# Sparse attention scores from three products of rounded query and key parts

## The chip, the cores and the metric

The kernel runs on one NeuronCore of a Trainium2 chip. The metric is the time of one execution on the device in microseconds (us). TensorE (PE in the profile) multiplies matrices into PSUM, VectorE (DVE), ScalarE (ACT) and GpSimd (POOL) work elementwise, SyncE (SP) issues transfers. Each engine runs its own queue in program order, and they meet at semaphores.

## The reference, cut to what matters

The program is a trunk of two layers on 512 tokens of width 1024: a gated DeltaNet mixer and a SwiGLU network, then a sparse attention mixer and another SwiGLU network. All of it is float32. The change lies in the attention of the second layer, whose core is:

```python
q = (c_q @ w_uq).reshape(B, S, DSA_HEADS, DSA_QK_DIM)        # 16 heads of 64
...
q_lat = jnp.einsum('bqhd,hdc->bqhc', q_b, w_uk)
s = jnp.einsum('bqhc,bqkc->bqhk', q_lat, kv_sel).astype(jnp.float32) * (DSA_QK_DIM ** -0.5)
s = jnp.where(valid[:, :, None, :], s, -jnp.inf)
p = jax.nn.softmax(s, axis=-1).astype(kv_sel.dtype)
o_lat = jnp.einsum('bqhk,bqkc->bqhc', p, kv_sel)
o = jnp.einsum('bqhc,hcv->bqhv', o_lat, w_uv)
```

Each query attends to 128 keys that an indexer has picked, from itself backwards. The kernel computes the scores against all keys up to the query's block and masks those not picked, and it multiplies the latents with `w_uk` first, so that queries and keys meet as vectors of 64 per head.

## The kernel before, in words

Queries `q_t` and keys `k_t` (L253, L255) are float32 tiles of 128 lanes x 8 head pairs x 512 tokens: lanes 0 to 63 hold one head of a pair, lanes 64 to 127 the other. There are 8 head pairs `i` and 4 query blocks `b` of 128 tokens; block `b` needs (b + 1) x 128 keys. A unit `u = 4 i + b` is one block of one pair.

For each unit TensorE computes the scores of both heads into two PSUM banks (`att_scores`, L2843). VectorE adds the mask and takes the row maximum (`masked`, L2958), ScalarE takes the exponentials (`att_exps`, L2855), TensorE transposes them (`turn`, L2868), ScalarE and VectorE copy one head each out of PSUM (`turned_out`, L2944 and L2946), and TensorE multiplies with the values (`values`, L2880). In TensorE's program step `t` is: scores of unit t, transposes of unit t-3, values of unit t-4. Once a pair there are the sums of the exponentials: VectorE's reciprocal and its rounded parts (L2972 to L2975), a transpose (L2888), ScalarE's copy, a broadcast product (L2894), VectorE's scaling (L2981), ScalarE's rounding `o_t_hi` (L2935) and VectorE's remainder `o_t_lo` (L2988). The order on every engine is written out by hand. Waits that matter here: scores of unit u wait until unit u-2 is masked (two pairs of banks), masking of unit u waits for the transposes of unit u-3, and the transposes of unit u wait until the copies of unit u-1 are out.

The first two units are computed inside `dsa_v_pe`, ahead of the last two of eight products that make the value tile `v_tok` (L2759 copies it out). At that time VectorE is at the indexer's top-k (MAX8 in L2819, MATCH_REPLACE in L2822), and the masking of unit 0 comes behind it.

All large products of the kernel use fp32r, a rounded form of float32: a number is split into a rounded part hi (written as F32R by a copy) and a remainder lo (a subtraction), and hi·hi + hi·lo + lo·hi is summed. The scores and the values of the attention are multiplied in plain float32 instead.

GpSimd makes the remainders of the first half of the output weights during the attention (`out_split`, L395, one after each of ScalarE's four `out_split_act` in steps 6, 10, 14 and 18), then rounds the second half (`out_hi_pool`, L705), whose remainders VectorE makes behind the attention. Behind it TensorE runs the output product (`pe_out`, L782 to L784). `qi_t` (L292) holds the indexer's queries in the place `h_base`, used until the last indexer logits.

Of the kernel before, what the change touches and what calls it, by code (L numbers as in the profile page):

```python
# [14 lines left out]
F32R = mybir.dt.float32r  # L15
ALU = mybir.AluOpType
# [3 lines left out]
P = 128  # L20
# [58 lines left out]
def build_trunk(nc, x, c, ada_w, ada_b, norm_g, ffn_w_in, ffn_w_out,  # L79
# [3 lines left out]
    _, S, D = x.shape  # L83
    DC = D // P
    NB = S // P
# [6 lines left out]
    AH, DH, LAT = dsa_w_uk.shape[1:]  # L92
    LC = LAT // P
    IH = dsa_w_qidx.shape[2] // DH
# [18 lines left out]
    with ExitStack() as ctx:  # L113
# [3 lines left out]
        def fixed(name, shape, dt=F32, at=None):  # L117
            size = 4
            for n in shape[1:]:
                size *= n  # L120
            size = (size + 31) // 32 * 32
            if at is None:
                at = place[0]
                place[0] += size
                assert place[0] <= nc.sbuf_usable_end, name
            t = nc.alloc_sbuf_tensor_at(name, shape, dt, offset=at)
            return t
# [48 lines left out]
        h_base = place[0]  # L176
# [75 lines left out]
        q_at = dsa.at  # L252
        q_t = dsa("q_t", [P, 8, S])  # L253
        k_at = dsa.at
        k_t = dsa("k_t", [P, 8, S])  # L255
# [34 lines left out]
        CB = [cb_gdn, cb_late, cb_late, cb_late]  # L290
        LATE = [late_gdn, late_ffn, late_dsa, late_ffn]
        qi_t = fixed("qi_t", [P, 4, S], at=h_base)  # L292
        mask = fixed("mask", [P, NB, S], at=h_base + 8192)
        v_tok = fixed("v_tok", [P, NB, 1024], at=h_base + 16384)
        relu = fixed("relu", [P, IH, S], at=ada_base)
# [3 lines left out]
        ps = ctx.enter_context(nc.psum_tensor("ps", [P, 8, S], F32))  # L299
# [3 lines left out]
        def sem(name):  # L303
            if name not in sems:
                sems[name] = ctx.enter_context(nc.semaphore(name))
            return sems[name]
# [16 lines left out]
        def f32(t):  # L323

            return t.bitcast(F32)
# [66 lines left out]
        def split(eng, ops, q, s, kc=8, src=None, dst=None):  # L392
            eng.wait_ge(hi_done, q * 4 + s + 1)
            lo, hi = (split_tile(w, s, kc) if dst is None else dst(w) for w in (w_lo, w_hi))
            ops.tensor_tensor(lo, raw_tile(s, kc) if src is None else src, f32(hi),  # L395
                              ALU.subtract).then_inc(lo_done, 1)
# [191 lines left out]
        def pool_root(pool, n):  # L588
            pool.wait_ge(sem("row_made"), 1 + 16 + n + 1)
            nc.gpsimd.tensor_tensor(rinv[:, NB * n:NB * n + NB], var[:, 0:NB], half[:, 0:NB], ALU.pow)\  # L590
                .then_inc(sem("row_root"), 1)
# [31 lines left out]
        def pool_first_root(pool):  # L623
            pool.wait_ge(sem("row_made"), 1)
            nc.gpsimd.tensor_tensor(row_rinv[:, 0, :], row_var[:, 0, :], half[:, 0:NB], ALU.pow)\
                .then_inc(sem("row_root"), 1)
# [55 lines left out]
        def out_views(m, q, s):  # L682

            if q == OUT_Q[m]:
                return raw_half(s), lambda w: w[:, s, :]
            late = LATE[m]
            if OUT_K[m] == DC:
                return raw_half(s), lambda w: late[0 if w is w_hi else 1][:, s, :]
            return flat(raw[0][:, :, :])[:, s * S:(s + 1) * S], \
                lambda w: late[0 if w is w_hi else 1][:, s // 2, (s % 2) * S:(s % 2 + 1) * S]  # L690
# [5 lines left out]
        def out_split(eng, ops, m, q, s):  # L696
            src, dst = out_views(m, q, s)
            split(eng, ops, q, s, src=src, dst=dst)
# [924 lines left out]
        def gdn_pool(pool):  # L1623

            load_ada(pool, 0, 4)
            load_ada(pool, 0, 5)
            load_ada(pool, 0, 6)
            load_ada(pool, 0, 7)
            pool_k_root(pool)
            load_ada(pool, 0, 8)  # L1630
            load_ada(pool, 0, 9)
            pool_strict(pool)
            for m in range(UNITS):
                pool_eu(pool, m)
            pool.wait_ge(sem("eu_made"), UNITS)
            nc.gpsimd.memset(xq[0:32, :, 32:64], 0.0).then_inc(sem("x_zero"), 1)
            pool_lower(pool)
# [133 lines left out]
        def states_pool(pool):  # L1771
            pool.wait_ge(sem("lower_cut"), 3)
            for m in range(UNITS):
                if m >= 3:
                    o_low(pool, m - 3)
                o_normed(pool, m)
            for m in range(UNITS - 3, UNITS):
                o_low(pool, m)
            pool.wait_ge(sem("h_made"), DC + UNITS)
# [754 lines left out]
        AT_QI, AT_Q, AT_UK, AT_K, AT_V = 0, 4, 12, 20, 28  # L2534
# [301 lines left out]
        def att_scores(pe, u):  # L2836
            i, b = u // NB, u % NB
            n = (b + 1) * P
            if u >= 2:
                pe.wait_ge(sem("nmax_made"), 2 * u - 2)  # L2840
            for a in range(2):
                lanes = slice(DH * a, DH * a + DH)
                last = nc.tensor.matmul(ps[:, 2 * (u % 2) + a, 0:n], q_t[lanes, i, b * P:(b + 1) * P],  # L2843
                                        k_t[lanes, i, 0:n], start=True, stop=True)
            last.then_inc(sem("s_mm"), 1)

        def att_exps(act, u):
            i, b = u // NB, u % NB
            n = (b + 1) * P
            if b == 0 and i >= 2:  # L2850
                act.wait_ge(sem("rsum_made"), i - 1)
            for a in range(2):
                act.wait_ge(sem("nmax_made"), 2 * u + a + 1)
                part = s_m[:, u % 3, a, 0:n]
                nc.scalar.activation(part, part, ACT.Exp, bias=nmax[:, 2 * (u % 3) + a:2 * (u % 3) + a + 1],  # L2855
                                     scale=-1.0, accum_out=psum_p[:, i % 2, 2 * b + a:2 * b + a + 1])\
                    .then_inc(sem("p_made"), 1)
# [184 lines left out]
        @block.gpsimd  # L3042
        def _(pool):
            ch = Chain(pool, sem("pool_chain"))

            def fill(t, value, *cuts):

                ch(nc.gpsimd.memset(t, value))
                for compare, other, base, pattern, channel in cuts:
                    ch(nc.gpsimd.affine_select(out=t, in_=t, compare_op=compare, fill=other, base=base,  # L3050
                                               pattern=pattern, channel_multiplier=channel))

            fill(ident[:, :], 0.0, (ALU.not_equal, 1.0, 0, [[-1, P]], 1))
            ch(nc.gpsimd.memset(ones[:, :], 1.0))
            nc.gpsimd.memset(half[:, :], -0.5).then_inc(sem("consts"), 1)
            for u in conv_u:
                ch(nc.gpsimd.memset(u[:, 0:3], 0.0))
            pool_first_root(pool)
            fill(upto[:, :], 1.0, (ALU.is_ge, 0.0, 0, [[1, P]], -1))
            ch(nc.gpsimd.memset(causal[:, :], 0.0))  # L3060
            nc.gpsimd.affine_select(out=causal[:, :], in_=causal[:, :], compare_op=ALU.is_ge, fill=-BIG, base=0,
                                    pattern=[[-1, P]], channel_multiplier=1).then_inc(sem("consts"), 1)
            gdn_pool(pool)
            states_pool(pool)
            load_ada(pool, 0, 10)
            pool_out(pool, 0)
            first_seven_pool(pool)
            pool_out(pool, 1)
            pool_root(pool, 0)
            pool.wait_ge(sem("small_sum"), 2)  # L3070
            nc.gpsimd.tensor_tensor(mean[:, :], mean[:, :], half[:, 0:NB], ALU.pow).then_inc(sem("small_root"), 1)
            pool_root(pool, 1)
            ch(nc.gpsimd.memset(r_parts[:, :, :], 0.0))
            for s in range(4):
                dsa_split_pool(pool, 2, s)
            pool.wait_ge(sem("lat_made"), 2 * LC)
            picked = tmp[0:40, 0, :].rearrange("p (b n) -> p b n", b=NB)
            ch(nc.gpsimd.memset(picked, 0.0))
            for base in (0, -32):
                ch(nc.gpsimd.affine_select(out=picked, in_=picked, compare_op=ALU.not_equal, fill=1.0, base=base,  # L3080
                                           pattern=[[-2, NB], [-1, 2], [0, DH]], channel_multiplier=1))
            nc.gpsimd.tensor_copy(pick[0:40, :, :], picked).then_inc(sem("consts"), 1)
            for s in range(4):
                out_split(pool, nc.gpsimd, 2, Q_DSA_OUT, s)
            for s in range(4):
                out_hi_pool(pool, Q_DSA_OUT + 1, s)
            pool_out(pool, 2)
            seven_pool(pool, 1)
            pool_out(pool, 3)
# [132 lines left out]
```

## Time and profile before

| | us |
|---|---|
| median of the runs (3) | 1359.1 |
| lowest and highest | 1358.92, 1359.27 |
| the profiled execution, its own time | 1357.8 |
| its span | 1356.1 |
| TensorE busy | 1294.5 (95%) |
| VectorE busy | 910.8 (67%) |
| ScalarE busy | 606.4 (45%) |
| GpSimd busy | 160.2 (12%) |

The profile is of one execution. The span is what the trace covers; the execution's own time is 1.7 us longer. The busy time of an engine says nothing on what ends last in a stage: for this the windows (busy time of each engine in a stretch, with the granted clock of TensorE, 1.00 being full) and the chain of waits are read. Ends of matmuls are modelled, and a matmul's duration holds its way through the array, so what counts is how far apart successive ones start.

### The profile page before, as it was taken

How to read it: one execution, taken by the hardware profiler on the slowest of the kernel's cores; microseconds unless marked ns; L12 is line 12 of the kernel's file. 1: busy time of each engine (PE TensorE's matmuls, PEld its weight loads, DVE VectorE, ACT ScalarE, POOL GpSimd, SP SyncE). 2: the span in 40 equal slices, each digit the busy share in tenths (PEclk: the TensorE clock that was granted, in tenths of full speed). 3: DMA queues.
4: the chain of work that ended last, by engine and by line, in shares of the span. 5: the costliest groups of instructions: out<-in, count | busy, mean ns of one | idle time of the engine just before them, and what ended most of it. 6: DMA issues, size and time to landing. Idle time of an engine off the chain costs nothing. (4 is left out here: it accounts for less than half of the span.)

```text
span 1356.1 us, 18327 instructions
## 1 busy us (share of the span) xinstructions
PE 1294.5 (95%) x6915; PEld 1062.6 (78%) x6915; DVE 910.8 (67%) x1588; ACT 606.4 (45%) x1141; POOL 160.2 (12%) x172
## 2 busy tenths in 40 slices
PE   3799999999999999999999999999999999999998
PEld 3668788889887888887788876666888888888886
DVE  4878787647566888678875759877465474457245
ACT  3256774545453332233234655587353342333231
POOL 1001120104401111102000001231010001000000
PEclk9799999989999999999999999999999999999999
DMA  9644523110508896879643120001136368336321
GB/s 323 201 166 149 193 63 94 64 62 1 187 31 323 225 241 241 242 217 242 244 166 94 39 79 32 31 32 33 62 108 174 102 145 217 111 76 155 95 92 63
DMA packets 111913, 183.56 MB, mean 135 GB/s; under 512 B 9933, under 2 KB 74714, under 8 KB 111578
## 3 DMA queue, kind: packets, MB, share of 16 engines
q1 hardware_dynamic: 87930, 107.01, 24.1%
q0 software_dynamic: 23904, 75.50, 20.1%
q8 instruction: 49, 0.80, 0.2%
q14 instruction: 30, 0.25, 0.1%
HBM read 178.31 MB, written 4.19 MB: 135 GB/s over the span
## 5 line engine op out<-in xcount | busy, mean ns | idle before, releaser
L411 PE MATMUL ps<-h_hi,w_hi 128*128 128x512 f32 x872 | 344.5, 395 | 0.4 <-ACT tmp L1066 0.4
L413 PE MATMUL ps<-h_hi,w_lo 128*128 128x512 f32 x872 | 341.3, 391 | 0.0
L412 PE MATMUL ps<-h_lo,w_hi 128*128 128x512 f32 x872 | 341.0, 391 | 0.0
L395 DVE TENSOR_TENSOR w_lo<-raw,w_hi 128x1024 fp32r<-128x1024 f32 x140 | 170.6, 1223 | 153.9 <-ACT w_hi L389 153.0
L413 PEld LDWEIGHTS ps<-h_hi,w_lo 128*128 128x128 f32 x872 | 164.7, 189 | 35.0
L411 PEld LDWEIGHTS ps<-h_hi,w_hi 128*128 128x128 f32 x872 | 164.9, 189 | 33.8 <-issue 0.5
L412 PEld LDWEIGHTS ps<-h_lo,w_hi 128*128 128x128 f32 x872 | 165.0, 189 | 33.5
L389 ACT ACTIVATE w_hi<-raw 128x1024 fp32r<-128x1024 f32 (+1 forms) x142 | 148.2, 1051 | 29.5 <-DMA raw<-in_ffn_w_in_dram 23.5
L514 DVE SCALAR_TENSOR_TENSOR ada_acc<-ada_in,c_act,ada_acc 128x512 f32<-128x512 f32 x154 | 115.6, 750 | 4.2
L2291 ACT ACTIVATE silu_g<-ps 128x512 f32<-128x512 f32 x44 | 26.1, 593 | 120.3 <-PE ps L413 110.9
L1072 DVE SCALAR_TENSOR_TENSOR tmp<-conv_u,conv_t,tmp 128x512 f32<-128x512 f32 x72 | 54.1, 752 | 35.6 <-ACT tmp L1066 33.5
L376 POOL DMA_DIRECT2D ada_in<-in_ada_w_dram x40 | 31.6, 815 | 285.5 <-DVE ada_acc L514 256.1
L2350 DVE TENSOR_TENSOR tmp<-silu_g,ps 128x512 f32<-128x512 f32 x44 | 30.2, 686 | 42.0 <-PE ps L413 41.5
L2056 DVE TENSOR_TENSOR w_lo<-raw,w_hi 128x1024 fp32r<-128x1024 f32 x32 | 38.4, 1222 | 22.9 <-ACT w_hi L2050 22.9
L2086 ACT ACTIVATE g_hi<-tmp 128x512 fp32r<-128x512 f32 x16 | 10.1, 633 | 90.1 <-DVE tmp L2098 90.1
L2050 ACT ACTIVATE w_hi<-raw 128x1024 fp32r<-128x1024 f32 x32 | 33.7, 1055 | 25.2 <-PE ps L2229 25.2
L2089 ACT ACTIVATE g_hi<-tmp 128x512 fp32r<-128x512 f32 x16 | 10.1, 634 | 73.0 <-DVE diag L2109 73.0
L2958 DVE CUSTOM_DVE_ANT_0 s_m<-ps,mask 128x128 f32<-128x128 f32 (+3 forms) x64 | 28.9, 489 | 19.2 <-PE ps L2868 16.3
L2147 DVE TENSOR_TENSOR y_ffn<-y_ffn,ps 128x512 f32<-128x512 f32 x48 | 32.9, 686 | 13.0 <-PE ps L2229 10.8
L2227 PE MATMUL ps<-w_hi,g_hi 128*128 128x512 f32 x96 | 37.7, 392 | 4.0 <-issue 2.6
L2855 ACT ACTIVATE s_m<-s_m,nmax 128x128 f32<-128x128 f32 (+3 forms) x64 | 35.3, 553 | 10.2 <-DVE nmax L2958 9.3
L988 POOL TENSOR_TENSOR row_rinv<-row_var,half 128x1 f32<-128x1 f32 x16 | 8.7, 546 | 262.2 <-DVE row_var L915 262.2
(429 smaller groups left out, 2601.5 us busy)
## 6 DMA issues: line engine op xcount, KB each, us to landing
raw<-in_ffn_w_in_dram SPq DMA_DIRECT2D x44, 1024.0 KB, 6.8
ada_in<-in_ada_w_dram POOLq DMA_DIRECT2D x40, 1024.0 KB, 7.0
raw<-in_gdn_w_in_dram SPq DMA_DIRECT2D x16, 1024.0 KB, 5.8
x_sum<-in_ffn_w_out_dram POOLq DMA_DIRECT2D x10, 1024.0 KB, 11.3
ada_in<-in_ffn_w_out_dram POOLq DMA_DIRECT2D x10, 1024.0 KB, 8.6
raw<-in_ffn_w_out_dram POOLq DMA_DIRECT2D x8, 1024.0 KB, 8.5
raw<-in_ffn_w_out_dram SPq DMA_DIRECT2D x12, 512.0 KB, 3.8
ada_in<-in_ada_w_dram SPq DMA_DIRECT2D x4, 1024.0 KB, 9.4
```

What stands on the lines that cost most here:

```text
L389: nc.scalar.activation(split_tile(w_hi, s, kc) if dst is None else dst(w_hi), raw_tile(s, kc) if src is None else src, ACT.Copy).then_inc( ...
L395: ops.tensor_tensor(lo, raw_tile(s, kc) if src is None else src, f32(hi), ALU.subtract).then_inc(lo_done, 1)
L411: nc.tensor.matmul(out_, hi[:, k, :], r_hi[:, k, :], start=k == 0, stop=False)
L412: nc.tensor.matmul(out_, hi[:, k, :], r_lo[:, k, :], start=False, stop=False)
L413: last = nc.tensor.matmul(out_, lo[:, k, :], r_hi[:, k, :], start=False, stop=k == kc - 1)
L514: ins = nc.vector.scalar_tensor_tensor(ada_sum(j)[:, :], slab_place(j)[b][:, k, :], cc, ada_sum(j)[:, :], ALU.mult, ALU.add)
L1072: ins = nc.vector.scalar_tensor_tensor(conv_a[n % 2], conv_u[n % 2][:, j:j + S], conv_t[:, j, channel(n):channel(n) + 1], conv_a[n % 2], A ...
L2050: nc.scalar.activation(w_hi[:, s, :], src, ACT.Copy).then_inc(hi_done, 1)
L2056: nc.vector.tensor_tensor(w_lo[:, s, :], src, f32(w_hi[:, s, :]), ALU.subtract).then_inc(lo_done, 1)
L2147: nc.vector.tensor_tensor(y, y, src, op).then_inc(sem("seven_read"), 1)
L2227: nc.tensor.matmul(out_, f_hi, hi, start=fresh and k == 0, stop=False, skip_group_check=True)
L2855: nc.scalar.activation(part, part, ACT.Exp, bias=nmax[:, 2 * (u % 3) + a:2 * (u % 3) + a + 1], scale=-1.0, accum_out=psum_p[:, i % 2, 2 * ...
```

## The change

The scores are computed as q_hi·k_hi + q_hi·k_lo + q_lo·k_hi in fp32r instead of one float32 product. The product of the two remainders is left out. For every unit there are so six matmuls, three for each head, instead of two.

GpSimd makes the parts of pair `i` in `parts_pool`: two casts into `qk_hi` (a double buffer of two pairs in the place of `qi_t`) and two subtractions into `qk_lo`, which lies on `q_t` and `k_t` themselves, so that q_t is overwritten by its own remainder. It waits until the query and key of the pair are there, and for the buffer: for pairs 0 and 1 until the last indexer logits are done, later until the scores of pair i-2 are done. TensorE's unit with b = 0 waits for the parts of its pair. In GpSimd's program the parts of pairs 0 and 1 come ahead of the output weights, those of pairs 2 to 5 each ahead of one of the four `out_split`, and those of pairs 6 and 7 ahead of `out_hi_pool`.

```diff
+        qk_hi = fixed("qk_hi", [P, 4, S], F32R, at=h_base)
+        qk_lo = [fixed(f"qk_lo{x}", [P, 8, S], F32R, at=at) for x, at in enumerate((q_at, k_at))]
...
-            for a in range(2):
-                lanes = slice(DH * a, DH * a + DH)
-                last = nc.tensor.matmul(ps[:, 2 * (u % 2) + a, 0:n], q_t[lanes, i, b * P:(b + 1) * P],
-                                        k_t[lanes, i, 0:n], start=True, stop=True)
+            if b == 0:
+                pe.wait_ge(sem("parts_lo"), 2 * i + 2)
+            q_hi, k_hi = qk_hi[:, 2 * (i % 2), :], qk_hi[:, 2 * (i % 2) + 1, :]
+            q_lo, k_lo = qk_lo[0][:, i, :], qk_lo[1][:, i, :]
+            for x, (q, k) in enumerate(((q_hi, k_hi), (q_hi, k_lo), (q_lo, k_hi))):
+                for a in range(2):
+                    lanes = slice(DH * a, DH * a + DH)
+                    last = nc.tensor.matmul(ps[:, 2 * (u % 2) + a, 0:n], q[lanes, b * P:(b + 1) * P], k[lanes, 0:n],
+                                            start=x == 0, stop=x == 2)
             last.then_inc(sem("s_mm"), 1)
+
+        def parts_pool(pool, i):
+
+            pool.wait_ge(sem("proj_out"), AT_Q + i + 1)
+            pool.wait_ge(sem("proj_out"), AT_K + i + 1)
+            if i < 2:
+                pool.wait_ge(sem("logit_mm"), 3 * IH)
+            else:
+                pool.wait_ge(sem("s_mm"), NB * (i - 1))
+            for x, t in enumerate((q_t, k_t)):
+                nc.gpsimd.tensor_copy(qk_hi[:, 2 * (i % 2) + x, :], t[:, i, :]).then_inc(sem("parts_hi"), 1)
+            for x, t in enumerate((q_t, k_t)):
+                pool.wait_ge(sem("parts_hi"), 2 * i + x + 1)
+                nc.gpsimd.tensor_tensor(qk_lo[x][:, i, :], t[:, i, :], f32(qk_hi[:, 2 * (i % 2) + x, :]),
+                                        ALU.subtract).then_inc(sem("parts_lo"), 1)
...
+            for i in range(2):
+                parts_pool(pool, i)
             for s in range(4):
+                parts_pool(pool, s + 2)
                 out_split(pool, nc.gpsimd, 2, Q_DSA_OUT, s)
+            for i in range(6, 8):
+                parts_pool(pool, i)
```

## Rows read from the trace of the kernel before

**Rows 1.** The page, busy time (share of the span) and instructions of TensorE.
```profile
PE 1294.5 (95%) x6915; PEld 1062.6 (78%) x6915; DVE 910.8 (67%) x1588; ACT 606.4 (45%) x1141; POOL 160.2 (12%) x172
```
**Rows 2.** Windows: length, busy us of PE, PEld, DVE, ACT, POOL; clock, DMA.
```profile
870.00:880.00 10.00, 7.34 (x42) 3.80 (x44) 4.98 (x25) 7.68 (x26) 0.00 (x0) 0.83 0.01 2
898.70:908.00 9.30, 9.19 (x83) 5.95 (x81) 6.96 (x26) 8.08 (x25) 2.36 (x1) 1.00 0.13 53
```
**Rows 3.** Chain that ended last, one head pair: start us, us, what.
```profile
902.33 0.37 PE ps L2868 x2
...
905.80 0.12 issue
...
911.74 0.37 PE ps L2868 x2
...
913.14 0.42 PE ps L2843 x4
```
**Rows 4.** Timeline of PE, score sets: start us, us, what [idle before].
```profile
907.50 0.92 PE L2843 MATMUL ps<-k_t,q_t 64*128 64x384 f32 x4
...
913.07 0.49 PE L2843 MATMUL ps<-k_t,q_t 64*128 64x128 f32 x4
...
882.51 1.13 PE L2843 MATMUL ps<-k_t,q_t 64*128 64x512 f32 x4
```
**Rows 5.** Chain and timeline, fp32r matmuls of 512 and of 256 columns.
```profile
951.24 0.23 PE ps L783
...
959.86 0.23 PE ps L782
...
760.40 0.28 PE L428 MATMUL ps<-h_hi,w_hi 128*128 128x256 f32 x1
760.52 0.28 PE L430 MATMUL ps<-h_lo,w_hi 128*128 128x256 f32 x1
```
**Rows 6.** Timeline of PE, matmuls of 128 columns.
```profile
900.76 0.55 PE L2894 MATMUL ps<-rsum_t,pick 40*128 40x128 f32 x3
...
908.34 1.09 PE L2868 MATMUL ps<-ident,s_m 128*128 128x128 f32 x8
```
**Rows 7.** Timeline of ACT and DVE ahead of block 2's transposes.
```profile
905.41 0.36 ACT L2944 ACTIVATE p_t<-ps 128x256 f32<-128x256 f32 x1
905.54 0.69 DVE L2988 TENSOR_TENSOR o_t_lo<-o_sb,o_t_hi 128x512 fp32r<-128x512 f32 x1
...
906.58 0.42 DVE L2958 CUSTOM_DVE_ANT_0 s_m<-ps,mask 128x256 f32<-128x256 f32 x1 [0.35 <-PE ps L2868]
```
**Rows 8.** Timeline and windows, score sets of pair 0, blocks 2 and 3.
```profile
871.75 3.29 PE L2843 MATMUL ps<-k_t,q_t 64*128 64x384 f32 x8 [2.37 <-ACT v_tok L2759]
...
872.00:873.00 1.00, 1.00 (x4) 0.59 (x6) 0.00 (x0) 0.67 (x4) 0.00 (x0) 0.50 0.00 0
...
874.00:875.00 1.00, 1.00 (x5) 0.04 (x1) 0.49 (x4) 0.95 (x3) 0.00 (x0) 0.58 0.00 0
```
**Rows 9.** Timeline of POOL, and its casts by line: ns min/median/max.
```profile
855.51 0.61 POOL L3082 CAST pick<-tmp 40x512 fp32r<-40x512 f32 x1
...
902.66 2.36 POOL L395 TENSOR_TENSOR w_lo<-raw,w_hi 128x1024 fp32r<-128x1024 f32 x1 [7.05 <-ACT w_hi L389]
...
L705 POOL CAST late_dsa<-raw x4: 1042/1044/1511, 914.4 to 920.4; 128x1024 fp32r<-128x1024 f32 x4
```
**Rows 10.** Timeline, first score sets and VectorE's first split behind the stage.
```profile
865.50 0.93 PE L2843 MATMUL ps<-k_t,q_t 64*128 64x128 f32 x8
...
952.91 4.62 DVE L395 TENSOR_TENSOR late_dsa<-raw,late_dsa 128x1024 fp32r<-128x1024 f32 x4
```
**Rows 11.** VectorE by line, ns min/median/max: with GpSimd at work, and without.
```profile
L2988 DVE TENSOR_TENSOR o_t_lo<-o_sb,o_t_hi x8: 691/692/1023, 896.1 to 952.3; 128x512 fp32r<-128x512 f32 x8
...
L2819 DVE MAX8 best<-tmp x7: 678/682/685, 841.0 to 854.5; 128x8 f32<-128x512 f32 x7
...
L2819 DVE MAX8 best<-tmp x8: 694/695/696, 856.8 to 867.5; 128x8 f32<-128x512 f32 x8
```

## The prediction

> **What bounds the kernel now.** I read the page's first line and the granted clock first: one core, span 1356.1 us, TensorE busy 95% [rows 1]. The change touches only the scores of the sparse attention (L2843), so the next view is the table of windows over that stage, from about 866 to 947 us. In the steady part TensorE is busy for 9.19 of 9.30 us, VectorE for 6.96 and ScalarE for 8.08; the start of the stage alone, 870 to 880 us, shows TensorE idle (7.34 of 10 us) and at a lower clock (0.83) [rows 2]. The chain of waits says the same: over a whole head pair it runs through TensorE alone, score sets, transposes, products with the values, again score sets, with one piece of 0.12 us that is "issue" [rows 3]. A pair takes 9.41 us (902.33 to 911.74, the transposes of block 0 of two successive pairs) [rows 3]. So time that the score matmuls save in blocks 2 and 3 is first seen at the end of the span, unless another loop takes over.
>
> **What the trace shows of the score sets.** A set is one query block of one head pair: a product for each of two heads, on lanes 0 to 63 and 64 to 127, recorded as four instructions. From first start to last end they take 0.49, 0.92 and 1.13 us for 128, 384 and 512 keys [rows 4]. The slope is 0.213 us per 128 keys, which at the granted clock of 1.00, the 2.4 GHz level, is four streams of 128 columns (4 x 128 / 2.4 = 213 ns) for both heads together; 0.28 us are left as a constant, and a set of 256 keys comes to 0.70. Four passes in all, and not eight, means that the two heads' matmuls run side by side and each full-precision product streams its keys four times.
>
> **What a rounded product costs.** fp32r matmuls of 512 columns follow each other by 0.227 us (951.24 to 959.86 in 38 steps) and those of 256 columns by 0.12 us [rows 5]. That is one stream each, plus 13 ns. With 128 columns the weight load is what shows: three fp32r matmuls of 128 columns take 0.55 us, 0.18 each with the last one's way out; eight transposes with as many columns take 1.09, 0.14 each [rows 6]; without that tail I estimate 0.11 to 0.14. No row shows an fp32r matmul on half the lanes, so that the pairs stay side by side is my reading of the full-precision sets.
>
> **The change, part by part.**
> Scores: two products per set (four streams for both) become six (three streams for both). With the constant of 0.28 us kept and three steps of n/2.4 plus 13 ns: 512 keys 0.96 instead of 1.13 (-0.17), 384 keys 0.80 instead of 0.92 (-0.12), 256 keys 0.64 instead of 0.70 (-0.06). Without the 13 ns, which the full-precision sets don't show, it is -0.21, -0.16 and -0.11. For 128 keys three weight loads stand in a row where there were two: +0.05 at 0.11 each, up to +0.15 at 0.14.
> Blocks 0 and 1 together are so about +0.03 us, and I count them at nothing: ahead of the transposes of block 2 TensorE is already waiting. The piece of "issue" at 905.80 is 0.12 us long, ends at 905.92, and ScalarE's copy p_t (L2944) of the block before runs 905.41 + 0.36 = 905.77 [rows 3, 7]. The transposes wait for that copy's semaphore, and the copy stands on ScalarE behind the exponentials and the rounding o_t_hi, which began with the transposes of block 0. What blocks 0 and 1 gain or lose within 0.12 us disappears in this gap. If the cover were gone they would cost 0.03 a pair.
> Blocks 2 and 3 lie behind it, on TensorE's own path: -0.29 to -0.37 us a pair, -0.33 taken. For pairs 1 to 7 this is 7 x 0.33 = 2.3 us (2.0 to 2.6).
> Pair 0, blocks 2 and 3: they start at 871.75, when the last v_tok copy has come, after 2.37 us of idle TensorE, and run at half clock (0.50 from 872 to 873) [rows 8]. The eight instructions take 3.29 us, of which the streams are 4 x 896 / 1.2 GHz = 2.99. Three streams are 2.24: -0.75. The transposes behind them then start at about 874.3, ahead of the rise of the clock (0.58 from 874 to 875, so it came near 874.8), and lose some of it: -0.6 taken.
>
> GpSimd: per pair two casts and two subtractions of 128x512. A cast with 512 elements a partition takes 0.61 us, one with 1024 1.04; a subtraction with 1024 takes 2.36, so one with 512 about 1.2 [rows 9]. That is 3.6 us a pair, 29 us in all, on an engine that is busy for 2.4 of 9.3 us [rows 2]. Pair i's parts may start when the last score set of pair i-2 is done and are wanted by the first set of pair i; by the chain that is 902.33 to 913.14, 10.8 us [rows 3]. Ahead of them stands at most one out_split (2.36 us): 6.0 of 10.8 us, so no set waits. Pairs 0 and 1: GpSimd is free at 856.12 (855.51 + 0.61), so the parts of pair 0 are there at about 859.8, and the first sets start at 865.50 [rows 9, 10]. If GpSimd were only done at 866 it would be queued ahead of the last two value products on TensorE, which have 2.37 us of idle time behind them: still nothing.
> What is queued behind GpSimd's new waits: the out_splits (L395), each released by ScalarE's w_hi after 7.05 us of idleness [rows 9], and the casts of the second half of the output weights, which are delayed from 914 us to about 926. Those are read by VectorE only after its last o_lo, from 952.91 on [rows 10]: nothing. The raw transfers behind out_split go out as before.
> VectorE: in the top-k before the stage a MAX8 of 512 took 682 ns beside GpSimd's subtractions and 695 without them [rows 11]: nothing for the parts of pairs 0 and 1. In the stage o_t_lo (L2988) took 692 ns, and 1023 the one time a GpSimd cast ran beside it, and that cast 1511 instead of 1044 [rows 9, 11]. So I allow +0.33 us on one VectorE instruction a pair; behind it VectorE is idle for 0.35 us (905.54 + 0.69 to 906.58) [rows 7]. Nothing on the path, at a hair's breadth.
> The page "SBUF — State Buffer" of the Trainium skill (section "SBUF: two separate sides") says that a VectorE operation with two SBUF inputs and a GpSimd operation that reads SBUF exclude each other for a whole instruction. The 1023 ns agree with that in kind. By that rule the wait could last a whole GpSimd subtraction, which is the third rival below and would make the sum 1362.2 instead of 1356.2.
> Nothing else moves: no DMA is added, and from 950.8 us on everything hangs on the end of the stage.
>
> **The sum.** -2.3 - 0.6 = -2.9 us. The profiled execution's span of 1356.1 becomes 1353.2; its own time of 1357.8 becomes 1354.9. It lies 1.3 us under the median of the runs, 1359.1, so the median becomes 1356.2. Within 0.2%, 2.7 us, a measurement of this kernel can't tell a difference from none, so the forecast lies just at that border.
>
> **Rivals.**
> 1. The loop over ScalarE and VectorE takes over, chance 0.24. For: ScalarE is busy for 8.0 of 9.3 us, the 0.12 us gap is already its doing, and VectorE starts each block's masking only behind TensorE's transposes [rows 2, 3, 7]. Against: behind blocks 2 and 3 neither is late. A third of the 2.3 us and the 0.6 at the start would be left, some 1.2 us: 1357.9.
> 2. The pairs don't run side by side with fp32r, chance 0.08, slower. Six streams stand where four did: per pair of heads +0.4, +0.2, +0.3 and +0.4 us for blocks 0 to 3, about 1.3 less the gap of 0.12, times 7 is 8.4, and at half clock 2 x 896 / 1.2 = 1.5: +10 us, 1369. It decides as soon as more than a third of each step is serial. Against: the slope of the full-precision sets.
> 3. GpSimd holds VectorE up, chance 0.12, slower. Two VectorE instructions per pair have both inputs in SBUF (L2988 and the small one of L2975). If o_t_lo waits for a whole subtraction of 1.2 us instead of 0.33, it passes the idle time of 0.35 by 0.85 us in each of seven pairs, 6.0 us, less the 2.9 gained: 1362.2. It decides from 0.35 + 0.33 = 0.7 us of waiting on.
> 4. The short sets cost nothing and ScalarE's loop is loosened with them, chance 0.06: blocks at -0.37 and -0.1 a pair, 3.3 + 0.75: 1355.0.
> The forecast has 0.50 (1355.5 to 1357.1). That the parts come late I take into rival 3; the margin is 4.8 us.
>
> **Chances and range.** The forecast's own band lies across the border of 1356.4 and is split 0.34 to 0.16. Faster: 0.34 + 0.06 + a few of rival 1's, 0.42. Slower: rival 2 and most of rival 3, 0.17. The rest, 0.41, is same. The range runs from rival 4 to rival 3 with their rounding, 1354.7 to 1362.5, and leaves out rival 2 and little more.
>
> **What would show it.** Right: sets of 0.54 to 0.64, 0.64, 0.80 and 0.96 us; about 9.08 us between the block 0 transposes of successive pairs; the first two long sets 2.5 instead of 3.29 us; GpSimd near 6 us busy in a pair; no TensorE wait on a GpSimd subtraction. Wrong: sets near 1.5 us for 512 keys (rival 2), the issue gap ahead of block 2 growing past 0.12 us or o_t_lo above 1.1 us (rivals 1 and 3), or a period that stays at 9.4 us with shorter sets.

## The result, and the profile after

The changed kernel is slower by 0.4%: a median of 1362.8 us over 13 runs (1357.7 to 1370.5) against 1359.1 us for the kernel before in as many (1354.9 to 1361.3), a ratio of 1.0037 with a 95% interval of 1.0025 to 1.005. The forecast was 1356.2 us, in a range of 1354.7 to 1362.5: the time lies just above the range and moved the other way. In a later group of runs, side by side on one chip, the same two kernels stood at 1.0043 (1.0029 to 1.0057). Of all the runs below a single one, of 1859 us in the experiment "Another instruction in the mask's place", was in a slow state and is not in the ratios.

The first lines of the page after:
```profile
span 1358.3 us, 18502 instructions
...
PE 1292.3 (95%) x6979; PEld 1067.6 (79%) x6979; DVE 923.4 (68%) x1588; ACT 605.7 (45%) x1141; POOL 190.4 (14%) x204
```
TensorE has 2.2 us less to do than in [rows 1], VectorE 12.6 us more with the same number of instructions, GpSimd 30.2 us more. Since no instruction of VectorE was added, something made old ones longer: 6.8 us of it is the instruction shown next, most of the rest the small `r_parts` instructions inside the attention (last section). Timeline of GpSimd and of VectorE in the changed kernel (start us, us, engine, line, what), just ahead of the last eight top-k rounds:
```profile
851.94 0.61 POOL L3104 CAST pick<-tmp 40x512 fp32r<-40x512 f32 x1
852.50 0.62 POOL L2863 CAST qk_hi<-q_t 128x512 fp32r<-128x512 f32 x1
853.05 0.62 POOL L2863 CAST qk_hi<-k_t 128x512 fp32r<-128x512 f32 x1
853.64 1.29 POOL L2866 TENSOR_TENSOR qk_lo<-q_t,qk_hi 128x512 fp32r<-128x512 f32 x1
...
858.51 1.28 POOL L2866 TENSOR_TENSOR qk_lo<-k_t,qk_hi 128x512 fp32r<-128x512 f32 x1
...
852.82 7.19 DVE L2828 TENSOR_SCALAR mask<-score 128x384 f32<-128x384 f32 x1
860.04 0.69 DVE L2821 MAX8 best<-tmp 128x8 f32<-128x512 f32 x1
```
VectorE's instruction that writes the mask of block 2 takes 7.19 us. GpSimd's eight instructions for pairs 0 and 1 run from 852.50 to 859.79 without a gap; the mask instruction is issued at 852.82 and is done 0.2 us after the last of them. In the kernel before the same instruction takes 0.363 us (line view: duration ns min/median/max, first and last start):
```profile
L2826 DVE TENSOR_SCALAR mask<-score x1: 363/363/363, 856.4 to 856.4; 128x384 f32<-128x384 f32 x1
```
It started at 856.45, a third of a microsecond after GpSimd's last cast, which ended at 856.12 [rows 9]. In the changed kernel the new run of GpSimd instructions begins where that cast ends.

Behind the mask everything waits: the other eight rounds, the masking of unit 0, the exponentials, the last copies of v_tok, and with them TensorE. TensorE's windows (length, busy us of PE, PEld, DVE, ACT, POOL, then clock, DMA share, GB/s) and the timeline line of the first new set:
```profile
874.94 0.69 PE L2850 MATMUL ps<-qk_hi 64*128 64x384 f32 x2 [9.10 <-ACT v_tok L2761]
...
877.00:880.00 3.00, 2.86 (x16) 1.56 (x12) 2.10 (x9) 2.54 (x8) 2.29 (x3) 0.50 0.00 0
880.00:883.00 3.00, 3.00 (x17) 2.11 (x17) 0.73 (x6) 1.53 (x8) 1.34 (x2) 0.50 0.00 0
883.00:886.00 3.00, 3.00 (x27) 2.08 (x27) 2.05 (x9) 1.90 (x6) 0.00 (x0) 0.87 0.00 0
```
TensorE is idle for 9.10 us where it was 2.37 [rows 8], and the granted clock is at its lower level, 1.2 GHz, until about 883.8, where before it was back near 874.8.

The score sets themselves, in the steady part, for 128, 384 and 512 keys (timeline of PE; the three lines of a set are its three products, each with both heads' matmuls):
```profile
889.00 0.33 PE L2850 MATMUL ps<-qk_hi 64*128 64x128 f32 x2
889.16 0.28 PE L2850 MATMUL ps<-qk_lo,qk_hi 64*128 64x128 f32 x2
889.28 0.28 PE L2850 MATMUL ps<-qk_hi,qk_lo 64*128 64x128 f32 x2
...
910.91 0.44 PE L2850 MATMUL ps<-qk_hi 64*128 64x384 f32 x2
911.18 0.34 PE L2850 MATMUL ps<-qk_lo,qk_hi 64*128 64x384 f32 x2
911.36 0.34 PE L2850 MATMUL ps<-qk_hi,qk_lo 64*128 64x384 f32 x2
...
886.71 0.50 PE L2850 MATMUL ps<-qk_hi 64*128 64x512 f32 x2
887.05 0.40 PE L2850 MATMUL ps<-qk_lo,qk_hi 64*128 64x512 f32 x2
887.28 0.40 PE L2850 MATMUL ps<-qk_hi,qk_lo 64*128 64x512 f32 x2
```
From first start to last end that is 0.56, 0.79 and 0.97 us, against 0.49, 0.92 and 1.13 in [rows 4]. The two heads' matmuls do run side by side.

The chain of waits gives the pair period and the ends of the stage (start us, us, what):
```profile
887.68 0.37 PE ps L2890 x2
...
896.58 0.38 PE ps L2890 x2
...
905.73 0.38 PE ps L2890 x2
...
942.40 0.38 PE ps L2890 x2
...
953.22 0.43 PE ps L784
```
Six periods from 887.68 to 942.40 are 9.12 us each on average. The same view of the kernel before:
```profile
883.64 0.37 PE ps L2868 x2
...
940.00 0.38 PE ps L2868 x2
...
950.81 0.43 PE ps L782
```
That is 9.39 us each; a single one of them is in [rows 3]. The first period is the shortest in both (8.90 and 9.27); the other five are 9.16 and 9.42.

Where the time went, in this one execution, counted from the first score set (865.50 in [rows 10], 861.93 after, so that what differs ahead of the stage, 3.57 us here, is left out). The stage ends at 950.81 before and 953.22 after: +5.98 us. The mask is +6.82. The two long sets of pair 0 take 2.61 instead of 3.29 us, -0.68, but the transposes and sets behind them run at half clock up to 883.8, so that the block 0 transposes at 887.68 are 0.85 us later against the set start than before. The six full periods give back 6 x 0.27 = 1.64. 6.82 + 0.85 - 1.64 = 6.0; the 0.85 has the 0.68 already in it. This is one execution. By the medians the loss is 3.7 us, which is near the mask's 6.8 less the 2.9 that were forecast as gain.

### The profile page after: what moved, and what is told of

Its sections match the earlier page's. It is cut to its first block and busy times, and to the rows that moved or that the text cites. A ratio compares the mean times of both kernels' runs of the same rounds, so it can differ in the third digit from the quotient of the medians.

```text
span 1358.3 us, 18502 instructions
## 1 busy us (share of the span) xinstructions
PE 1292.3 (95%) x6979; PEld 1067.6 (79%) x6979; DVE 923.4 (68%) x1588; ACT 605.7 (45%) x1141; POOL 190.4 (14%) x204
## 5 line engine op out<-in xcount | busy, mean ns | idle before, releaser
L2352 DVE TENSOR_TENSOR tmp<-silu_g,ps 128x512 f32<-128x512 f32 x44 | 30.2, 686 | 42.5 <-PE ps L415 42.0
```

## The experiments

Theory A: GpSimd's unbroken run for pairs 0 and 1 keeps VectorE's mask instruction out for its whole length; the score products themselves are worth what was forecast. Theory B: the three products and the added wait cost the time, and the mask is an accident of one execution.

All edits are to the changed kernel unless said otherwise. The kernels of a group ran on one chip, each against runs of the kernel before on it. Ratios are to that kernel, with their 95% intervals.

**Late parts.** VectorE's chain stands at 435 once the mask of block 2 is made, so GpSimd starts its parts behind it.
```diff
+            pool.wait_ge(sem("dve_chain"), 435)
             for i in range(2):
                 parts_pool(pool, i)
```


> GpSimd's parts of pairs 0 and 1 wait until VectorE's mask of block 2 is made (about 3.6 us of GpSimd time for each pair then lie beside the last eight top-k rounds). Theory A (in the changed kernel the 7.19 us of that mask instruction, against 0.36 before, are GpSimd's eight instructions shutting it out): the instruction takes 0.36 us again, TensorE's idle time ahead of pair 0's block 2 falls from 9.1 to about 2.4 us, the half clock ends earlier, and the time is about 2.5 us under the kernel before, 0.998 of it, some 7 us under the changed one. Theory B (the three fp32r products and the new wait are what costs): the time stays 3 to 5 us over the kernel before, 1.003.

0.9986 (0.9970 to 1.0002), 1356.5 us. The mask and the idle time of TensorE are back at the values of before:
```profile
L2828 DVE TENSOR_SCALAR mask<-score x1: 361/361/361, 856.1 to 856.1; 128x384 f32<-128x384 f32 x1
...
  ACT v_tok L2761: 2.3, 1
...
870.00:880.00 10.00, 7.88 (x74) 5.64 (x74) 6.42 (x28) 8.70 (x29) 3.64 (x4) 1.00 0.01 2
```
(line view, what ended the sets' idle time, and a window.) In this execution the clock stayed at 1.00 from 866 to 896 us. Everything but the place of GpSimd's first eight instructions is as in the changed kernel, so theory B falls: it asked for 1.003, above the whole interval.

**Parts alone.** The scores are one float32 product again, of the remainders:
```diff
-            for x, (q, k) in enumerate(((q_hi, k_hi), (q_hi, k_lo), (q_lo, k_hi))):
-                for a in range(2):
...
+            for a in range(2):
+                lanes = slice(DH * a, DH * a + DH)
+                last = nc.tensor.matmul(ps[:, 2 * (u % 2) + a, 0:n], f32(qk_lo[0][lanes, i, b * P:(b + 1) * P]),
+                                        f32(qk_lo[1][lanes, i, 0:n]), start=True, stop=True)
```


> GpSimd makes all parts as in the changed kernel, but the scores are one float32 product of each head's remainders (the products with the rounded parts are left out, so the scores are not those of the reference). Theory A: mask instruction about 7 us, half clock for longer, score sets of 0.49 to 1.13 us and 9.4 us a pair as before: about 8 to 9 us over the kernel before, 1.006. Theory B: as the kernel before, 1.000.

1.0057 (1.0038 to 1.0075), 1365.6 us: the whole loss, and by the middle value more than the changed kernel's 1.0037, as theory A has it, though the two intervals overlap.
```profile
L2828 DVE TENSOR_SCALAR mask<-score x1: 7159/7159/7159, 854.3 to 854.3; 128x384 f32<-128x384 f32 x1
...
  ACT v_tok L2761: 9.1, 1
```

**Scores alone.** All calls of `parts_pool` and the wait for them are gone; ScalarE writes queries and keys as F32R:
```diff
-            q_hi, k_hi = qk_hi[:, 2 * (i % 2), :], qk_hi[:, 2 * (i % 2) + 1, :]
-            q_lo, k_lo = qk_lo[0][:, i, :], qk_lo[1][:, i, :]
+            q_hi, k_hi = q_r[:, i, :], k_r32[:, i, :]
+            q_lo, k_lo = q_hi, k_hi
```


> GpSimd makes no parts; ScalarE writes queries and keys rounded, and the scores are three fp32r products of the rounded parts with themselves (the remainders are left out, so the scores are three times those of rounded operands). Theory A: mask instruction 0.36 us, sets as in the changed kernel, pairs 9.1 us apart, 2 to 3 us under the kernel before, 0.998. Theory B: 3 to 5 us over it, 1.003.

0.9989 (0.9975 to 1.0004), 1356.0 us. Mask 361 ns, pairs 9.14 us apart (892.54 to 938.26 in five). With the parts on GpSimd the same five periods are 9.16 us in the changed kernel and 9.16 to 9.18 in the kernels with late parts and with gaps, so the parts cost 0.02 to 0.03 us a pair there. The execution that was profiled was one of the longest of its kernel, 1361.5 us, and shows one way in which single executions differ: TensorE was idle for only 2.3 us, and yet the clock stayed down for some 10 us.
```profile
871.00:874.00 3.00, 3.00 (x18) 1.59 (x14) 2.45 (x9) 2.37 (x9) 0.00 (x0) 0.56 0.00 0
...
877.00:880.00 3.00, 3.00 (x19) 2.08 (x17) 1.78 (x8) 1.62 (x5) 0.00 (x0) 0.50 0.00 0
880.00:883.00 3.00, 3.00 (x24) 2.46 (x24) 1.55 (x5) 1.55 (x4) 0.00 (x0) 0.73 0.00 0
```

**Pair 1 late.** The wait of the first experiment stands between the parts of pair 0 and those of pair 1.
```diff
+            parts_pool(pool, 0)
+            pool.wait_ge(sem("dve_chain"), 435)
+            parts_pool(pool, 1)
```


> The parts of pair 0 are made at once, those of pair 1 wait until the mask of block 2 is made. If VectorE's instruction is held until GpSimd's unbroken run of instructions ends (theory A in its strong form): about 3.5 us instead of 7.2, and a time between the changed kernel and the one with both pairs late, about 1 us over the kernel before. If it is held for one GpSimd instruction at most (weak form): under 1.7 us. If something else than GpSimd's run holds it: 7 us as in the changed kernel.

1.0013 (0.9998 to 1.0027), 1360.6 us. Half the run, half the wait:
```profile
856.40 1.29 POOL L2866 TENSOR_TENSOR qk_lo<-k_t,qk_hi 128x512 fp32r<-128x512 f32 x1
...
854.37 3.53 DVE L2828 TENSOR_SCALAR mask<-score 128x384 f32<-128x384 f32 x1
```
GpSimd's four instructions end at 857.69, the mask at 857.90. It is the length of GpSimd's run that the mask instruction waits for, the strong form of theory A: four instructions, not one.

**Another instruction in the mask's place.**
```diff
+            if b == 2:
+                ch(nc.vector.match_replace(mask[:, b, 0:(b + 1) * P], best[:, b % 2, :],
+                                           score[b % 2][:, 0:(b + 1) * P], 0.0))
+                return
```


> As the changed kernel, but the mask of block 2 is written by a MATCH_REPLACE8 over the same 384 elements (one SBUF input and SBUF output as the TENSOR_SCALAR has, 0.53 us in the top-k rounds, so slower per element), at the same place beside GpSimd's run. The comparison of the scores with the top-k threshold is left out for block 2, so its mask is not the reference's. Theory C (only an instruction that VectorE runs faster than one element a cycle is shut out, as the TENSOR_SCALAR with 384 elements in 0.36 us, while MAX8 and MATCH_REPLACE8 are not): 0.55 us, and 6 to 7 us less than the changed kernel. Theory D (any VectorE instruction that starts fresh behind the top-k pair waits for the run): about 7 us, time as the changed kernel.

0.9975 (0.9960 to 0.9990), 1356.0 us: as theory C has it, and theory D falls. With GpSimd's run of eight beside it, unbroken from 856.44 on:
```profile
857.00 0.62 POOL L2867 CAST qk_hi<-k_t 128x512 fp32r<-128x512 f32 x1
...
856.84 0.54 DVE L2829 MATCH_REPLACE8 mask<-best,score 128x384 f32<-128x384 f32 x1
```
The slower instruction on the same 384 elements, from and to the same tiles, goes through at once in 0.54 us. The fast one, 0.36 us when alone, is the one that is kept out.

**Gaps.** Each of GpSimd's parts instructions waits for its predecessor's end.
```diff
                 nc.gpsimd.tensor_copy(qk_hi[:, 2 * (i % 2) + x, :], t[:, i, :]).then_inc(sem("parts_hi"), 1)
+                pool.wait_ge(sem("parts_hi"), 2 * i + x + 1)
             for x, t in enumerate((q_t, k_t)):
-                pool.wait_ge(sem("parts_hi"), 2 * i + x + 1)
...
                                         ALU.subtract).then_inc(sem("parts_lo"), 1)
+                pool.wait_ge(sem("parts_lo"), 2 * i + x + 1)
```


> As the changed kernel, but each of GpSimd's parts instructions waits for the end of the one before, so that a short gap lies between them. If VectorE's instruction is only kept out as long as GpSimd's next instruction starts before the last has ended: the mask takes at most about 1.6 us instead of 7.2 (its own 0.36 and the rest of one GpSimd instruction), and the time is about 5 us under the changed kernel, near 1.000 of the kernel before. If GpSimd holds on over the gaps: 7.2 us or more, and the time as the changed kernel or above.

0.9966 (0.9952 to 0.9980), 1355.0 us, better than the 1.000 expected.
```profile
854.27 0.62 POOL L2863 CAST qk_hi<-q_t 128x512 fp32r<-128x512 f32 x1
854.95 0.62 POOL L2863 CAST qk_hi<-k_t 128x512 fp32r<-128x512 f32 x1
855.66 1.29 POOL L2866 TENSOR_TENSOR qk_lo<-q_t,qk_hi 128x512 fp32r<-128x512 f32 x1
...
854.63 0.47 DVE L2828 TENSOR_SCALAR mask<-score 128x384 f32<-128x384 f32 x1
```
Two casts now start 0.68 us apart and last 0.62, where they were 0.55 apart. The mask, issued while the first cast runs, ends at 855.10 and takes 0.47 us instead of 7.19. Under a tenth of a microsecond between two GpSimd instructions is enough to let the mask instruction in.

**The order of ScalarE behind it.** TensorE's 2.3 us of idle time end with the v_tok copies, which stand behind the exponentials of unit 0 on ScalarE. Here those two copies come first, in the late-parts kernel and then in the kernel before.
```diff
             for j in range(8):
-                if j == 6:
-                    att_exps(act, 0)
                 proj_ready(act, AT_V + j)
...
+            att_exps(act, 0)
```


> As e1_late_parts, and ScalarE copies the last two v_tok tiles out ahead of the exponentials of unit 0 instead of behind them. TensorE's idle time before pair 0's block 2 (2.3 us) ends with the masking of unit 0 instead of with the copy, about 1.6 us earlier: about 1.6 us under e1_late_parts, 0.9975 of the kernel before; more where the shorter idle time spares a fall of the clock. If the idle time is bound by something else it stays at 0.9986.

> The kernel before with only the order of the last v_tok copies and the exponentials of unit 0 turned round, to split the gain of e6: about 1.6 us under the kernel before, 0.9988. If the gain of e6 needs the changed kernel's scores, 1.000 here.

0.9964 (0.9948 to 0.9980), 1354.1 us, and 0.9976 (0.9961 to 0.9991), 1355.5 us. Both gained some 0.1% more than expected. The idle time ahead of the long sets falls from 2.3 and 2.4 to 0.8 us in either. The new order gives its 0.2% to the old kernel too; with it, what is left for the scores is the difference of 0.9976 and 0.9964, within the intervals of both.

**Side by side.** Four kernels on one chip: gaps with the new order, gaps, late parts, and the changed kernel.

> e7_gaps with the v_tok copies ahead of the exponentials of unit 0. The scores' 1.6 us from pairs 1 to 7, 0.7 at the start and 1.1 to 1.6 of the order add up: 3.5 to 5 us under the kernel before, 0.9965, and 1 to 1.6 us under e10_gaps_again on the same chip. If the gaps between GpSimd's instructions cost something in the stage, it shows as a pair period over the 9.15 us of e1_late_parts.

> The kernel of e7_gaps once more, beside that of e1_late_parts on one chip. With the mask instruction at 0.47 against 0.36 us and the same pair period, both should be equal within 0.1%, 0.998 of the kernel before. If a run of GpSimd instructions without gaps also cost time inside the attention, this one would be 1 us or more the faster.

> The kernel of e1_late_parts once more, for the comparison with the gaps: 0.998 of the kernel before, 6 to 7 us under the changed kernel on the same chip.

> The changed kernel itself, on the chip of the three others: 1.0037 of the kernel before; the mask instruction 7.2 us in this execution too, since GpSimd's run starts behind its own work (pick) and VectorE's mask behind its own top-k, both at fixed places. If the mask's 7 us were an accident of one execution it would now be well below.

| kernel | ratio to before | 95% interval | median us |
|---|---|---|---|
| gaps, new order | 0.9974 | 0.9960 to 0.9989 | 1354.5 |
| gaps | 0.9981 | 0.9967 to 0.9996 | 1355.6 |
| late parts | 0.9962 | 0.9948 to 0.9976 | 1353.4 |
| changed kernel | 1.0043 | 1.0029 to 1.0057 | 1363.6 |

The changed kernel's mask took 7145 ns in this execution, so it is no accident. The new order is worth 1.2 us on top of the gaps here, less than the intervals can tell. Gaps and late parts were expected to be equal within 0.1%, 6 to 7 us under the changed kernel; they lie 2.3 us apart, 7.9 and 10.2 us under it. Gaps and late parts came out at 0.9966 and 0.9986 in their first groups and at 0.9981 and 0.9962 here, in the opposite order: I can't tell one from the other, and both are near 0.9974. The fastest by its ratio is the late-parts kernel, in one of its two groups; every version with gaps or with both pairs' parts late beats the changed kernel, and of their intervals all but that of the first late-parts run (up to 1.0002) lie under the kernel before.

## Why the prediction was wrong

By its own steps:

- What bounds the stage, and the path through TensorE: right for blocks 2 and 3. The sum of the steady part was 7 x 0.33 = 2.3 us; measured are 0.27 us a pair, 1.64 for the six whole periods, which would be 1.9 for seven. The sets came out at 0.56, 0.79 and 0.97 us where 0.54 to 0.64, 0.80 and 0.96 were forecast. The gap ahead of block 2's transposes held as said: from block 0's transposes (906.11) to those of block 2 (909.32) it is 3.21 us, against 3.22 by [rows 3] (902.33 + 0.37 to 905.92). TensorE's idle time ahead of them grew from 0.12 to 0.20 us, and it ends with ScalarE's p_t as before.
- Pair 0's long sets: 0.68 less while the clock was down, where 0.75 was worked out. That the return of the clock stays where it was, near 874.8, failed: behind 9.10 us of idle TensorE instead of 2.37 it came near 883.8.
- GpSimd's time: 0.61 and 1.28 us against 0.61 and 1.2, 30.2 us in all against 29, and no wait of TensorE ends with it. Right.
- **The step that failed** is the sentence on VectorE in the top-k: "nothing for the parts of pairs 0 and 1". It was read from MAX8, which has one input and runs slowly, and applied to all that VectorE does in that stretch. There is one other kind of instruction in it, the TENSOR_SCALAR that makes the mask, and it lies on the path that ends with the stage. It cost 6.8 us, more than twice the whole forecast gain of 2.9.
- The third rival had the right pair of engines and a time, 1362.2, close to the result, but the wrong instruction, place and size: it put seven waits of 0.85 us on o_t_lo inside the attention. There, o_t_lo did take up to 1.11 us, the sign that the prediction had named, but next to nothing was lost: over the same five periods 9.14 us a pair without the parts, 9.16 with them. That rival is refuted as the cause, in spite of its number.
- Rival 1 (ScalarE's loop takes over) is left with almost nothing. The two long sets of a pair are 0.13 and 0.16 us shorter, 0.29 together, and the pair 0.27: the prediction's version with the 13 ns a step was the right one, and 0.02 us a pair may be ScalarE's. (Its own time was added up wrongly: a third of 2.3 and the 0.6 are 1.4 us, so 1357.7 and not 1357.9.) Rival 2 is excluded by the sets.

With the mask out of the way the change does about what was forecast: 0.9986, 0.9966, 0.9981 and 0.9962 in four measurements of two kernels on three chips, 0.9974 in the mean or -3.6 us, against the -2.9 of the sum (0.9979).

The same page of the Trainium skill that the prediction drew on for two-input instructions, "SBUF — State Buffer", also says (section "Who interferes with whom") that a tensor_scalar can run in a mode that takes both of VectorE's port pairs, one of which is GpSimd's, and is then blocked. The prediction left that half out. The traces agree with it: 0.36 us for 384 elements alone, against 0.54 for MATCH_REPLACE8, and only the faster is kept out. By the page the second to issue waits until the first finishes; measured is more for the mask instruction, which waited for eight GpSimd instructions in the changed kernel and for four in the pair-1-late kernel.

## What to carry to other kernels

Before work is put on GpSimd "beside" VectorE, list every instruction that VectorE runs in that stretch with its rate, not only the most frequent one, and look for the fast kind (here a TENSOR_SCALAR from and to SBUF) on the path. If there is one, move GpSimd's run behind it, or make each GpSimd instruction wait for the end of the one before: both took 0.5 to 0.8% off the changed kernel. And if the total busy time of an engine rises with the same number of instructions, compare durations line by line before anything else.

## What the runs showed of the hardware

VectorE's TENSOR_SCALAR from and to SBUF, which takes 0.36 us for 384 elements where MATCH_REPLACE8 takes 0.54, was shut out by GpSimd for as long as GpSimd's instructions followed each other with overlapping ends: 7.19, 7.16 and 7.15 us for eight instructions, 3.53 for four, 0.47 with gaps of under 0.1 us, 0.36 without GpSimd. MAX8 and MATCH_REPLACE8 beside the same runs kept their 0.69 and 0.68 us.

Other VectorE instructions inside the attention were held too, but only for one GpSimd instruction and off the path. The small subtraction `r_parts` (L2975 before, L2997 here), which has two inputs in SBUF, had a median of 1064 ns against 168 before. Line view, then timeline of the changed kernel:
```profile
L2997 DVE TENSOR_TENSOR r_parts<-rsum,r_parts x8: 166/1064/1194, 884.7 to 947.8; 128x8 f32<-128x8 f32 x8
...
899.75 0.62 POOL L2863 CAST qk_hi<-q_t 128x512 fp32r<-128x512 f32 x1
900.30 1.09 POOL L2863 CAST qk_hi<-k_t 128x512 fp32r<-128x512 f32 x1
...
910.64 1.27 POOL L2866 TENSOR_TENSOR qk_lo<-q_t,qk_hi 128x512 fp32r<-128x512 f32 x1
911.87 1.27 POOL L2866 TENSOR_TENSOR qk_lo<-k_t,qk_hi 128x512 fp32r<-128x512 f32 x1
...
899.80 1.11 DVE L3010 TENSOR_TENSOR o_t_lo<-o_sb,o_t_hi 128x512 fp32r<-128x512 f32 x1
...
911.38 0.56 DVE L2996 CAST r_parts<-rsum 128x8 fp32r<-128x8 f32 x1
```
The cast of eight elements ends at 911.94, just behind the first GpSimd subtraction (911.91), though the next followed without a gap. With o_t_lo it is the same: it is held behind the first GpSimd cast (ended 900.37), done at 900.91, and now the second GpSimd cast takes 1.09 us instead of 0.62. So between two GpSimd instructions without a gap these two kinds of VectorE instruction got in, and the mask did not, though a run of eight has seven such places. What stays open is why. That it hangs on how fast VectorE runs an instruction rests on one comparison only, TENSOR_SCALAR against MATCH_REPLACE8.

The clock's part is a matter of chance to some extent. Over the 30 us from 866 to 896 the mean granted clock was 0.77 and 0.83 in the two profiles of the changed kernel, and 0.83 and 0.77 in the parts-alone and pair-1-late kernels, all four with 5.5 to 9.1 us of idle TensorE before. In the ten profiles with 2.5 us or less it was 1.00 in five, 0.94 in four and 0.83 in one (scores alone). A long pause so always cost clock here, a short one in half of the cases, and mostly less. In six of the fourteen profiles (the kernel before not among them) the clock fell once more between 943 and 960 us, at the end of the attention. The spread of single runs is not larger in the changed kernel: 6.4 us before and 12.7 after in the first group, but 6.8 and 7.6 side by side on one chip. Of the 13 runs of the changed kernel in the first group the three longest (1366.8 to 1370.5 us) have a mean clock of 0.981 and 0.982 and the other ten 0.984 to 0.986; in 30 runs of the kernel before on one chip there is no such order. The clock is so a part of the spread, not all of it.
